# Order of two groups of small products in nine gaps between weight products: pair products of HGRN scores ahead of products of the delta rule's inverse

## Time and profile before

| | |
|---|---|
| median of 3 runs | 3088.0 us (3086.55 to 3088.46) |
| the profiled execution | 3088.74 us |
| its span, first to last instruction | 3086.9 us |
| PE busy / DVE busy / ACT busy | 3005.9 / 2084.9 / 1491.8 us |
| granted TensorE clock, mean | 0.992 of full speed |
| a usual unit, `r_scores` to `r_scores` | 105.85 us |

### The profile page before, as it was taken

One profiled execution on the slowest core, in us unless ns is written; L12 is line 12 of the kernel. 1 busy time (PEld: TensorE's weight loads), 2 busy tenths in 40 slices (PEclk: granted clock), 3 DMA queues, 4 the chain that ended last, 5 costly groups with the idle time before them and its releaser, 6 DMA issues.

```text
span 3086.9 us, 50772 instructions
## 1 busy us (share of the span) xinstructions
PE 3005.9 (97%) x20316; PEld 2761.3 (89%) x20316; DVE 2084.9 (68%) x3164; ACT 1491.8 (48%) x2154; POOL 324.8 (11%) x512
## 2 busy tenths in 40 slices
PE   4999999999999999999979999999999999999998
PEld 4999999999998888888879999999999988888886
DVE  4877887787776545545558877877787765545554
ACT  5455445545555444444454455455545544444443
POOL 2220212022000000000012120221120000000000
PEclk9999999999999999999989999999999999999999
DMA  4555555555546666665625555555555566666654
GB/s 117 140 148 137 141 143 147 136 144 143 146 134 202 194 194 192 194 194 187 204 81 138 147 146 138 142 144 145 144 136 147 160 191 192 194 195 192 194 179 164
DMA packets 614108, 494.23 MB, mean 160 GB/s; under 512 B 18512, under 2 KB 496272, under 8 KB 613360
## 3 DMA queue, kind: packets, MB, share of 16 engines
q1 hardware_dynamic: 606800, 485.09, 54.0%
q0 software_dynamic: 6784, 4.70, 0.8%
q10 hardware_dynamic: 288, 1.18, 0.1%
HBM read 488.81 MB, written 2.10 MB: 159 GB/s over the span
## 4 chain that ended last, share of the span: by engine, by line
PE 69%; issue 26%; DVE 1%; ACT 1%; POOLq 1%; POOL 1%; DVEq 0%; DMA 0%; ACTq 0%; SPq 0%
PE PJ L1458 44%; PE GA L1458 6%; PE S L1458 6%; PE HA L1458 5%; PE RA L1458 3%; PE GB L1458 3%; POOL g_ms L513 0%; DMA lsel<-c_lsel 0%; POOLq L503 0%; POOL r_rs L509 0%; POOLq L501 0%; PE S L1651 0%; PE RA L1707 0%; ACTq L596 0%; ACT work L789 0%
## 5 line engine op out<-in xcount | busy, mean ns | idle before, releaser
L1000 DVE TENSOR_TENSOR w_lo<-raw_w,w_hi 128x1024 fp32r<-128x1024 f32 x912 | 1116.9, 1226 | 720.2 <-ACT w_hi L560 696.9
L560 ACT ACTIVATE w_hi<-raw_w 128x1024 fp32r<-128x1024 f32 x912 | 963.0, 1058 | 792.1 <-PE PJ L1458 338.9
L1458 PE MATMUL PJ<-h_hi,w_hi 128*128 128x256 f32 x3584 | 1047.3, 292 | 0.0
L1458 PE MATMUL PJ<-h_hi,w_lo 128*128 128x256 f32 x3584 | 1015.7, 283 | 0.0
L1458 PE MATMUL PJ<-h_lo,w_hi 128*128 128x256 f32 x3584 | 1015.1, 283 | 0.0
L1458 PEld LDWEIGHTS PJ<-h_hi,w_hi 128*128 128x128 f32 x3584 | 687.8, 192 | 11.9 <-issue 11.9
L1458 PEld LDWEIGHTS PJ<-h_lo,w_hi 128*128 128x128 f32 x3584 | 688.2, 192 | 0.0
L1458 PEld LDWEIGHTS PJ<-h_hi,w_lo 128*128 128x128 f32 x3584 | 686.9, 192 | 0.0
L1458 PE MATMUL PJ<-w_hi,h_hi 128*128 128x512 f32 x640 | 249.2, 389 | 1.9 <-DVE h_lo L1390 1.9
L1458 PE MATMUL PJ<-w_hi,h_lo 128*128 128x512 f32 x640 | 249.0, 389 | 0.0
L1458 PE MATMUL PJ<-w_lo,h_hi 128*128 128x512 f32 x640 | 249.0, 389 | 0.0
(11 more groups left out here) (397 smaller groups left out, 4212.9 us busy)
## 6 DMA issues: line engine op xcount, KB each, us to landing
raw_w<-w_in SPq DMA_DIRECT2D x704, 512.0 KB, 3.7
raw_w<-w_branch SPq DMA_DIRECT2D x128, 512.0 KB, 4.5
raw_w<-w_out SPq DMA_DIRECT2D x64, 512.0 KB, 3.7
raw_w<-s_glu_w SPq DMA_DIRECT2D x16, 512.0 KB, 4.8
ret_decay<-c_ret POOLq DMA_DIRECT2D x16, 128.0 KB, 3.1
work<-final_norm_w SPq DMA_DIRECT2D x2, 1024.0 KB, 7.7
out<-x_tok SPq DMA_DIRECT2D x4, 512.0 KB, 2.9
x_tok<-x ACTq DMA_DIRECT2D x1, 1024.0 KB, 8.0
```

The source lines that it names most:

```text
L560: A_(w_hi[i % RING][:, :, :], raw_w[i % RING][:, :, :], ACT.Copy).then_inc(hi_ready, 1)
L1000: TT(w_lo[i % RING][:, :, :], raw_w[i % RING][:, :, :], w_hi[i % RING][:, :, :].bitcast(f32), ALU.subtract).then_inc(raw_used[i % RING], 1)
L1458: return nc.tensor.matmul(o, w, m, start=start, stop=stop)
```

## The change

In eight of the gaps `h_pairs(stage)` is now issued before `g_tx(s)` or `g_txt(s)`, and in the ninth `h_cross()` before `g_txt(5)`. No instruction is added or removed. The orders of ACT, DVE, POOL and the DMA queues are as they were.

```
                     project(11)
+                    h_pairs(0)
                     g_txt(1)
-                    h_pairs(0)
                     project(12)
+                    h_pairs(1)
                     g_tx(2)
-                    h_pairs(1)
                     project(13)
+                    h_pairs(2)
                     g_txt(2)
-                    h_pairs(2)
                     project(14)
                     values(hv, hv_staged, 1)
+                    h_pairs(3)
                     g_tx(3)
-                    h_pairs(3)
                     project(15)
+                    h_pairs(4)
                     g_txt(3)
-                    h_pairs(4)
                     project(16)
+                    h_pairs(5)
                     g_tx(4)
-                    h_pairs(5)
                     project(17)
+                    h_pairs(6)
                     g_txt(4)
-                    h_pairs(6)
                     project(18)
+                    h_pairs(7)
                     g_tx(5)
-                    h_pairs(7)
                     project(19)
+                    h_cross()
                     g_txt(5)
-                    h_cross()
                     g_values()
                     project(20)
                     g_tx(6)
```

## The result

The changed kernel takes 3096.95 us (median of 8, 3095.59 to 3097.58) against 3088.01 (median of 8, 3086.55 to 3089.36). The ratio is 1.0028 with a 95% interval of 1.0018 to 1.0038: slower by 8.9 us. The forecast was 3097.4. The profiled execution took 3096.79, span 3094.9.

What follows compares the result with a forecast made beforehand. PE, busy 97% of the span, was taken as the bound, losing only where DVE's answers come late. Terms of 6.2 + 3.2 = 9.4 us against the median of 3088.0 gave 3097.4 us, range 3092.5 to 3101.0.

Steps and rivals of the forecast that it cites:

- PE's own time unchanged: In PE's gaps: the same products in either order take 1.35 us, so the direct effect is 0.
- Term 1: PE's r_scores waits for roped in every unit: 13 x 0.37 + 3 x 0.45 = 6.2 us.
- DVE's chain: DVE from invert(3) to rope(1), back to back for 19 us: all of it moves later by 0.45 us.
- Term 2: h_pairs(1), after project(12), waits for h_scores(0) in nine units, 0.36 us each: 3.2 us.
- `h_pairs(7)`: Waits for h_scores(6), 0.03 us or about 0.4 to 0.5 in two paused units; no further term, r_scores waits less.
- Rivals: Four alternative outcomes to the forecast: only r_scores waits, more waits, no change, or faster by over 0.2% (0.03).
- rival 3: Wait swallowed, by PE passing a held load or DVE's chain absorbing the shift: no change, 3088.0 us; chance 0.13.
- rival 2: More waits: h_pairs(1) late in all units and a few more DVE pauses, 13 us, 3101; chance 0.12.
- rival 1: Only r_scores waits, h_pairs(1) does not as the meeting with POOL moves: 3094.2 us; chance 0.12.

Runs made afterwards that it cites:

- e3: Changed kernel with the gaps after project(12) and project(15) put back, leaving the other seven swaps: 3087.92 us, ratio 1.0000.
- e4: Kernel before, PE's order untouched, with one more 128x256 product on DVE between h_scores(4) and s5_back(0): 3093.43 us, ratio 1.0017.
- e5: Changed kernel with DVE's s5_back(1) moved from before ahead(18) to behind ahead(19), so roped comes earlier: 3091.13 us, ratio 1.0009.
- e1: Kernel before with one swap only, h_pairs(4) ahead of g_txt(3) after project(15): 3093.83 us, ratio 1.0018.
- e6: Changed kernel with POOL's arithmetic of s5_matrices held until roped of the current unit: 3094.05 us, ratio 1.0019.
- e2: Kernel before with one swap only, h_pairs(1) ahead of g_tx(2) after project(12): 3090.06 us, ratio 1.0006.
- e7: Changed kernel with both the DVE move of s5_back(1) and POOL's s5_matrices arithmetic held until roped: 3089.58 us, ratio 1.0004.
- e8: Kernel before, PE's order untouched, with DVE's s5_back(1) moved from before ahead(18) to behind ahead(19): 3086.24 us, ratio 0.9993.

## Why the prediction was right

- *PE's own time unchanged.* Right: a gap of 1.34 us against 1.35, and seven swaps at 0.0 in e3.
- *Term 1, 6.2 us.* Right in place, count and size. All 16 units wait, 0.36 us where 0.37 was put, and 5.8 us when made alone. e4 and e5 show it from both sides: later by other work, it costs the same, and made earlier, it costs nothing.
- *DVE's chain.* The shift of 0.45 was 0.44. Two statements on the way were wrong: that ACT's later copies are hidden, and that DVE's idle time before `invert(3)` grows by 0.45. It stayed at 0.72. ACT's `copy_r(3)` comes later, hence the `w_hi` behind it, and the `w_lo` in front of the mask waited 1.21 us for that in unit 3 where it waited 0.31 (710.2 us over the run where it was 696.9). PE does not feel this, but DVE does. It cost nothing in the end, because `invert(3)` waits for `g_txt(3)` either way: in e1, where `g_tx(3)` is not moved, DVE is idle 1.17 us before `invert(3)`, and `r_scores` is as late.
- *Term 2, 3.2 us.* Place and size of one wait right (0.36), the number a little low, 11 of 16 units in the profile against nine. Alone it measured 2.0, and 3.2 in its trace. Its cause, argued before, is shown by e6.
- *`h_pairs(7)`.* Two visible waits, in two of the three units with a pause, and no term of their own, as put: in unit 2 `r_scores` is then idle 0.28 us only, where it is 0.72 in e1, which has no wait at `h_pairs(7)`.
- *Rivals.* A swallowed wait (rival 3) is refuted by e1 and e4: in both the stretch is longer by the whole wait, so the queue of TensorE did not get past a held load. More waits (rival 2) came in part, two more units and no more pauses. What rival 1 describes, term 1 without term 2, is what e1 makes, 3093.8; in the changed kernel term 2 is there.

What stays open is about 1 us: the waits counted make 9.9, the medians say 8.9, and the parts sum to 7.6. The traces place it. Each profiled execution against that of the kernel before, PE's loads, in us, once for the stages that set up the two layers (up to unit 0, and from `r_scores` of the first layer's last unit to unit 0 of the second) and once for everything else:

| | everything else | stages ahead of unit 0 |
|---|---|---|
| changed kernel | +9.9 | -1.9 |
| e1 | +5.8 | -0.4 |
| e2 | +3.2 | -2.0 |
| e3 | 0.0 | -1.1 |
| e4 | +5.6 | -0.3 |
| e5 | +5.1 | -1.5 |
| e6 | +6.6 | +0.3 |
| e7 | +5.7 | -0.2 |
| e8 | -0.9 | -1.6 |

In the first column the parts e1, e2 and e3 are 5.82 + 3.20 + 0.04 = 9.06 of 9.86. Of the other 0.8, 0.7 is the difference between 11 waits of `h_pairs(1)` and the eight long and two short ones of e2. The second column scatters by 2 us with no order in it, and only e6 has these stages longer than the profile of before. So the loss is accounted for within 0.1 us where the waits stand. That the forecast of 3097.4 came within 0.5 us of the median is in part luck: term 2 was put 0.7 too low and term 1 about 0.3 too high, and the stages ahead of the units, which the forecast takes as unchanged, scatter by more than that.

## What to carry to other kernels

On an engine that never seems to wait, order still matters through the engine that answers it: before moving a small group ahead of another, list for each group which answer it needs, when that comes, and how much later the group it is moved past will be answered. A shift of a few tenths of a us is free while some idle time on the other engine takes it up, and is paid in full at the next answer that was just in time. That answer can be in another branch of the work, 19 us on. So move only groups with slack (seven of nine here), and mend the tight answer first.

## What the hardware showed beyond that

A wait for a count of DVE cost PE the same at the front of a gap and in its middle, start for start, with 0.08 us from the end of DVE's row to PE's load. DVE's instructions with two operands in SBUF were stretched beside POOL's (0.59 against 0.43 us, the mask 0.68 against 0.41), and POOL's own small one beside DVE's `w_lo`, to 1.26 where 0.19 is usual. DVE also paused by 0.3 to 0.5 us for nothing that the profile shows. On the way to `roped` it did so in the same three units before and after, and at seven other places of the units, the same ones in both. In e4, whose DVE program is one instruction longer, the places are others (0.52 us of idle time in unit 3). What they are was not tried.
